# Eight divisions and orders of the five matmuls of a feed-forward tile

## The reference

```
def swiglu(x, w_gate, w_up, w_down):
    return (jax.nn.silu(x @ w_gate) * (x @ w_up)) @ w_down

for l in range(DEPTH):                      # DEPTH = 2
    x = x + 0.5 * swiglu(rms_norm(x, ffn1_norm[l]), *f1)   # w_gate, w_up: 1024 x 2816; w_down: 2816 x 1024
    x = x + mixer(rms_norm(x, mix_norm[l]))                # even layer: attention and gating; odd: convolution and latent attention
    x = x + 0.5 * swiglu(rms_norm(x, ffn2_norm[l]), *f2)
y = rms_norm(x, final_norm)
```

## Time and profile before

| | us |
|---|---|
| median of 3 runs | 2147.6 |
| lowest and highest of them | 2140.06, 2149.92 |
| the profiled execution | 2138.32 |
| its span, first to last instruction | 2136.6 |
| PE busy | 2085.3 (98%) |
| PEld busy | 2004.9 (94%) |
| DVE busy | 1168.0 (55%) |
| ACT busy | 800.5 (37%) |
| mean granted TensorE clock | 0.990 of full speed |

### The profile page before, as it was taken

One profiled execution on the slowest core, in us unless ns is written; L12 is line 12 of the kernel. 1 busy time (PEld: TensorE's weight loads), 2 busy tenths in 40 slices (PEclk: granted clock), 3 DMA queues, 4 the chain that ended last, 5 costly groups with the idle time before them and its releaser, 6 DMA issues.

```text
span 2136.6 us, 38050 instructions
## 1 busy us (share of the span) xinstructions
PE 2085.3 (98%) x14550; PEld 2004.9 (94%) x14550; DVE 1168.0 (55%) x1604; ACT 800.5 (37%) x1260; POOL 285.4 (13%) x290
## 2 busy tenths in 40 slices
PE   8999999999999999999999999999989899999997
PEld 8999999997999999999999999999834799999997
DVE  6553555557665435555553555556835365535544
ACT  5331333327356313334651333222334246513331
POOL 0000111300320000022000001503145320000012
PEclk9999999999999999999999999999999999999999
DMA  3222443212132322222232223322489422322231
GB/s 135 84 99 84 120 122 101 96 64 79 60 102 90 108 76 88 92 95 79 89 103 78 85 88 101 115 91 85 138 233 277 133 87 91 103 76 88 88 101 69
DMA packets 68708, 218.60 MB, mean 102 GB/s; under 512 B 10186, under 2 KB 22645, under 8 KB 68544
## 3 DMA queue, kind: packets, MB, share of 16 engines
q1 hardware_dynamic: 58864, 191.00, 27.4%
q0 software_dynamic: 9184, 24.80, 4.1%
q10 hardware_dynamic: 576, 1.67, 0.2%
HBM read 212.67 MB, written 5.78 MB: 102 GB/s over the span
## 4 chain that ended last, share of the span: by engine, by line
PE 91%; DVE 4%; ACT 2%; SPq 1%; DMA 1%; issue 1%; DVEq 0%; ACTq 0%
PE ps L661 17%; PE ps L660 16%; PE ps L659 15%; PE ps L681 15%; PE ps L662 13%; PE ps L663 11%; DVE rinv L1590 1%; PE ps L1103 1%; SPq L536 1%; DVE w_lo L1580 1%; PE ps L1035 1%; PE ps L1130 1%; DMA keys<-pool_kt 0%; DMA x<-xT 0%; ACT prob L1358 0%
## 5 line engine op out<-in xcount | busy, mean ns | idle before, releaser
L1246 ACT ACTIVATE w_hi<-raw 128x1024 fp32r<-128x1024 f32 (+2 forms) x298 | 335.2, 1125 | 580.4 <-PE ps L663 382.0
L661 PE MATMUL ps<-hx,w_hi 128*128 128x384 f32 x1408 | 469.3, 333 | 0.0
L659 PE MATMUL ps<-hx,w_hi 128*128 128x352 f32 x1408 | 451.2, 320 | 8.9 <-DVE w_lo L1580 4.0
L660 PE MATMUL ps<-hx,w_hi 128*128 128x352 f32 x1408 | 454.3, 323 | 0.0
L662 PE MATMUL ps<-hx,w_lo 128*128 128x288 f32 x1408 | 412.4, 293 | 0.0
L1580 DVE TENSOR_TENSOR w_lo<-raw,w_hi 128x1024 fp32r<-128x1024 f32 (+2 forms) x298 | 401.9, 1349 | 16.9 <-ACT w_hi L1246 16.6
L663 PE MATMUL ps<-hx,w_lo 128*128 128x256 f32 x1408 | 395.4, 281 | 0.0
L659 PEld LDWEIGHTS ps<-hx,w_hi 128*128 128x128 f32 x1408 | 265.5, 189 | 10.6 <-issue 5.9
L663 PEld LDWEIGHTS ps<-hx,w_lo 128*128 128x128 f32 x1408 | 265.1, 188 | 0.0
L661 PEld LDWEIGHTS ps<-hx,w_hi 128*128 128x128 f32 x1408 | 264.8, 188 | 0.0
L660 PEld LDWEIGHTS ps<-hx,w_hi 128*128 128x128 f32 x1408 | 264.7, 188 | 0.2
(11 more groups left out here) (332 smaller groups left out, 2990.2 us busy)
## 6 DMA issues: line engine op xcount, KB each, us to landing
raw<-gu SPq DMA_DIRECT2D x175, 512.0 KB, 3.7
raw<-down SPq DMA_DIRECT2D x64, 704.0 KB, 4.0
keys<-pool_kt SPq DMA_DIRECT2D x128, 144.0 KB, 4.2
vals<-pool_v POOLq DMA_DIRECT2D x128, 128.0 KB, 4.2
raw<-odd_in SPq DMA_DIRECT2D x21, 512.0 KB, 3.6
raw<-even_in SPq DMA_DIRECT2D x14, 512.0 KB, 3.6
raw<-even_out SPq DMA_DIRECT2D x8, 512.0 KB, 3.7
raw<-odd_out SPq DMA_DIRECT2D x8, 512.0 KB, 3.8
```

The lines of the kernel that those rows point to most:

```text
L659: pe.matmul(one, hi, rhs[:, t, 0:PIECE], start=opens, stop=False)
L660: pe.matmul(two, hi, rhs[:, t, PIECE:2 * PIECE], start=opens, stop=closes)
L661: pe.matmul(three, hi, rhs[:, t, 2 * PIECE:2 * T], start=opens, stop=False)
L1246: act.activation(w_hi[slot][:, 0:cols], raw[slot][:, 0:cols], ACT.Copy).then_inc(w_hi_done, 1)
```

## The change

The constants `PIECE` and `LOW_CUT` give way to a table. For each of the four stages it holds one entry for the gate-and-up part and one for the down part: the sizes of `one`, `two` and `three`, the cut between the two low-weight matmuls, the order of the five matmuls (0: `one`, 1: `two`, 2: `three`, 3: low weights into `one`, 4: low weights into `three`), and a number of columns by which `one` is moved away from the border of its bank. With such a move `one` and `two` no longer meet, and DVE adds `upper` to x in two operations instead of one.

```
-PIECE = 352
-LOW_CUT = 288
+PLAN = (((384, 352, 352, 288, (2, 4, 0, 3, 1), 0), (352, 352, 384, 288, (0, 3, 2, 1, 4), 0)),
+        ((512, 288, 288, 288, (0, 1, 2, 3, 4), 0), (384, 384, 320, 288, (0, 1, 2, 3, 4), 0)),
+        ((352, 352, 384, 272, (0, 1, 2, 3, 4), 0), (352, 352, 384, 288, (0, 1, 2, 3, 4), 32)),
+        ((352, 352, 384, 288, (0, 3, 2, 4, 1), 0), (288, 512, 288, 288, (0, 1, 2, 3, 4), 0)))
...
+        def pieces_of(plan, slot):
+            a, b, c, cut, order, shift = plan
+            return ps[:, 2 * slot, BANK - a - shift:BANK - shift], ps[:, 2 * slot + 1, 0:b], ps[:, 6 + slot, 0:c]
...
+                    for k in order:
+                        if k == 0:
+                            last = pe.matmul(one, hi, rhs[:, t, 0:a], start=opens, stop=False)
...
+                        if k == 4:
+                            last = pe.matmul(three[:, T + cut - a - b:c], lo, rhs[:, t, cut:T], start=False, stop=closes)
...
+                if plan[5]:
+                    dve.scalar_tensor_tensor(out=xm[:, 0:p0], in0=one, scalar=factor, in1=xm[:, 0:p0], op0=ALU.mult, op1=ALU.add)
+                    dve.scalar_tensor_tensor(out=xm[:, p0:T], in0=two, scalar=factor, in1=xm[:, p0:T], op0=ALU.mult, op1=ALU.add).then_inc(x_upper, 1)
+                else:
+                    dve.scalar_tensor_tensor(out=xm, in0=upper_of(plan, slot), scalar=factor, in1=xm, op0=ALU.mult, op1=ALU.add).then_inc(x_upper, 1)
```

More of the change, by code:

```diff
@@ L294, in decoder_step, with upper_of, lower_of, lower_count @@
         acc = [ps[:, 2 * s:2 * s + 2, :] for s in range(2)]
[L295 to L298, removed]
+        def pieces_of(plan, slot):
+            a, b, c, cut, order, shift = plan
+            return ps[:, 2 * slot, BANK - a - shift:BANK - shift], ps[:, 2 * slot + 1, 0:b], ps[:, 6 + slot, 0:c]
+        def upper_of(plan, slot):
+            a, shift = plan[0], plan[5]
+            at0 = (2 * slot + 1) * BANK - a
+            if shift:
+                return None
+            return ps_flat[:, at0:at0 + T]
+        def lower_of(plan, slot):
+            a, b, c = plan[0:3]
+            return ps[:, 2 * slot + 1, T - a:b], ps[:, 6 + slot, 0:c]
+        def lower_count(plan):
+            return plan[0] + plan[1] - T
         def sem(name):
@@ L644, in _, with wide_panel @@
         def _(pe):
-            def wide_panel(n, slot, rhs, tiles, wait_input=None, begin=True, end=True, first=False):
+            def wide_panel(n, slot, rhs, tiles, wait_input=None, begin=True, end=True, first=False, plan=None):
                 if begin:
@@ L651, in wide_panel @@
                         pe.wait_ge(acc_read, n - 1)
-                one, two, three = pieces[slot]
+                one, two, three = pieces_of(plan, slot)
+                a, b, c, cut, order, shift = plan
                 for t in tiles:
@@ L658, in wide_panel @@
                     closes = end and t == tiles[-1]
[L659 to L663, removed]
+                    for k in order:
+                        if k == 0:
+                            last = pe.matmul(one, hi, rhs[:, t, 0:a], start=opens, stop=False)
+                        if k == 1:
+                            last = pe.matmul(two, hi, rhs[:, t, a:a + b], start=opens, stop=closes)
+                        if k == 2:
+                            last = pe.matmul(three, hi, rhs[:, t, a + b:2 * T], start=opens, stop=False)
+                        if k == 3:
+                            last = pe.matmul(one[:, 0:cut], lo, rhs[:, t, 0:cut], start=False, stop=closes)
+                        if k == 4:
+                            last = pe.matmul(three[:, T + cut - a - b:c], lo, rhs[:, t, cut:T], start=False, stop=closes)
                 if end:
@@ L707, in ffn @@
             def ffn(start, f, norm):
+                gu, down = PLAN[f]
                 for c in range(CHUNKS):
```

67 lines of the change are left out of this document (36 added, 31 removed).

## The result

The changed kernel takes 2161.9 us (median of three runs, 2161.65 to 2165.82) against 2147.6 us before (2140.06 to 2149.92). The ratio is 1.0076, 95% interval 1.0043 to 1.0109: 14.3 us between the medians, 0.8% by the ratio, and slower by an interval that lies clear of no change. The time lies inside the predicted range and 8 us above the predicted 2154. The profiled execution took 2161.93 us, span 2160.3 us; the one before took 2138.32 us with 2136.6 us. From profile to profile the loss is therefore 23.7 us, more than between the medians. Why these two differ is a question of its own (the experiments `again` and `lowshift`).

The account below looks back on a forecast made before the run. PE was taken as the bound, busy 98% of the span. 1829 tiles at 4.0 ns more (7.3 us), less 1.0 us for 107 tiles, made 6.3 us: 2147.6 became some 2154 us, range 2137 to 2169.

Parts of the forecast that it names:

- The shift in f2's down part and its second addition: Feed-forward stage f2, down part: 0 for 176 tiles; DVE's divided addition 0.15 us more per panel, covered by other work.
- the middle value for the 1936 tiles without a row: Feed-forward parts with new sequences: 737.3 ns a tile, 4.0 more than now, taken between two rows of the old trace.
- rival 2: Feed-forward tiles: old sequence overlaps some losses, others pay 13.3 ns per matmul; 24.3 us more, 2172 us; chance 0.32.
- Rival 1: Feed-forward tiles: division and order don't matter, every part returns to 733.3 ns; 2147.6 or 2146.2 us; chance 0.13.
- Rival 3: Feed-forward tiles: faster, smaller matmul losses; all parts at 720 ns would save 27.2 us, 2120 us; chance 0.13.
- the same sum: Whole kernel: 6.3 us more, added to the profiled execution (2144.6 us) and to the median (2153.9 us).
- Slower by over 0.5%: Whole kernel: an outcome over 10.7 us slower, from an average of 5.9 ns a tile on; chance 0.35.

Follow-up runs that it names:

- again: The kernel before, unchanged, profiled a second time; the profiled execution took 2158.83 us.
- lowshift: The kernel before with only the low weights placed 32 columns further on in memory: 2144.91 us against 2145.74, ratio 0.9999.
- dear: The kernel before with four new entries (f0 down, f1 gate-and-up, f3 gate-and-up and down): 2157.93 us against 2147.67, ratio 1.0045.
- cheap: The kernel before with four new entries (f0 gate-and-up, f1 down, f2 gate-and-up and down): 2149.44 us against 2147.67, ratio 0.9998.
- uniform: A kernel with work left out or repeated and matmuls of one size in each part, five to a tile: 119.8 ns at 256 columns, 226.6 at 512.
- seq: A table with 16 entries; four parts had the old sequence of sizes by other pieces, orders and cuts: 740.0 or 746.7 ns a tile.
- uniform2: The matmuls of uniform with input or weights read some columns further on: 384 columns took 176.0 ns with weights moved by 32, 173.5 unmoved.

## Why the prediction was right, and where it was not

The place of the cost was right. PE is the bound, nothing changed but the distance between starts, and DVE, ACT and the waits added nothing. The shift in f2's down part and its second addition were put at 0 for the tiles, 0.15 us for a panel and covered: the tiles measure 733.3 ns, the two additions 873 ns, and PE enters the odd mixer as before. That the halves `dear` and `cheap` add up agrees with it.

The size was not. The step that failed is the middle value for the 1936 tiles without a row, 737.3 ns or 4.0 more than before. By the table they average 747.5 ns (733.3 plus 27.4 us over 1936 tiles), 14.2 more. The tiles were to lie between 725 and 747 ns; three parts lie above, at 753 to 755.5, and none below 733.3. By the marks the prediction set itself (mean near 737, or most at 746 and more) this is rival 2: 24.3 us had been worked out for it, 24.5 us are in the table. The value was the middle between the earlier trace rows, the undisturbed old entry, and the earlier trace rows, and no row said that a new entry would keep half of what the old one saves. The row that came nearest was the dearest: 13.3 ns for each matmul is 746.7 for a tile, and `uniform` finds 13.3 ns for five sizes by themselves.

Rival 2's mechanism holds in half. The old entry does save 13.3 ns of a tile, and the new ones, f2's down part aside, pay 6.7 to 22.2 more. It isn't the loss of one matmul that is saved: in the trace of the kernel before, the mean distances in the earlier trace rows are shorter than those in the earlier trace rows by 5.1, 1.6, 5.0 and 4.2 ns behind the first four matmuls and longer by 2.6 behind the fifth. Nor is it the sequence of sizes that saves it: the same sequence at other places has 740.0 and 746.7 (`seq`), and the old entry loses its saving in some parts and runs (`again`). Rival 1, by which division and order don't matter, falls by every table here. Rival 3 falls too; no part was under 733.3. The Trainium skill (TensorE: Matmul & The Clock Gate, Back-to-back issue gap) gives the distance that the prediction took from it, columns over 2.4 plus 2.5 ns, as that of an isolated matmul; for a stream of weight loads and matmuls, as here, it says that both set the distance. The trace has 13.3 ns and not 2.5 in such a stream even where all matmuls are alike, and a shorter weight load shortens the distance at 256 columns but not at 384 (`uniform`).

The medians moved by 14.3 us and not by 24 because the two profiles stand at different places among their runs: that of the kernel before is 9.3 us under its median, that of the changed kernel is its median. The prediction put the same sum on the median as on that short execution. What fills those 9.3 us in a median execution isn't shown, since none of the kernel before was profiled. Two things that can fill them are on record: parts in the long tile (14.1 us in `again`) and the odd mixer (6.6 us in `again`, 8.4 in `lowshift`, whose profile lies near that median with all but one part at 733.3). Only the first would mean that the new entries lose less against a median execution than the profiles say; that they do is not shown. The runs speak for it: those of the changed kernel lie within 6.6 us (eight runs) and those of `dear` within 3.6, those of `cheap`, `lowshift` and the kernel before within 13 to 21. The prediction had read in the earlier trace rows that a part keeps the length it fell into; it did not ask how often parts fall into the long one, nor how much else differs between executions.

So two errors stood against each other. From profile to profile the parts and the mixer cost 23.6 us and not 6.3, 17.3 more than forecast; 9.3 of that vanish between the medians, and 8 us are left in the result. That the time came so near is luck. Slower by over 0.5%, to which 0.35 had been given, is what the ratio says, though its interval reaches down to 0.43%.

What stays open is what decides between the lengths. It is a loss per matmul that is absent at the low clock (1360 ns for a tile's 1632 columns), changes with the place of the input and of the weights, did not depend on the output bank for 352 columns, and can settle at one of two values for the same program. Whether reads of the weights and of the input meet in one memory was not measured, and no run here shows what sets a part into the long tile.

## What to carry to other kernels

A profile of one execution may show the good one of several lengths: before a change to a tight stream is priced against it, take a second profile of the kernel before and read the period of each part, and the length of every other stage, in both. Where a stream of matmuls already has a loss below that of its single matmuls, a reordering without a reason from the trace more likely loses that than gains (over fifty entries here, and no gain), and the prior for an unseen order should be the full loss of each matmul. Many variants can be tried in one kernel if each part has its own and is read by its own period.

## What the hardware showed unexpectedly

- At a granted clock of 1.00 matmuls of one size lose 13.3 ns each for 256, 320, 384, 416 and 512 columns, whatever the size, but 11.7 for 288, 14.4 for 352, and 16 and 20 in panels by turns for 448 (`uniform`).
- The column at which an operand starts changes this: 384 columns lose 13.3 from column 0 and from 16, 15.9 from 32, and 16.0 with weights that start 32 columns further on; 512 columns lose 13.3 from 0 and 18.9 from 32 (`uniform2`).
- The same program part has a tile of 733.3 ns in one execution and of 746.7 in another, each held through nearly the whole part, at a granted clock of 1.00.
